# Three-term products over all 640 tokens in the dense projections of a two-layer trunk on one core

## The reference

```python
h = modulate(rms_norm(x, W['norm1_w'][l]), sh1, sc1)
# layer 0
qa, ka, va, qb, fa, fb, vb, gb = jnp.split(h @ w_in, offs, axis=-1)
...
y = jnp.concatenate([oa, ob], axis=-1) @ w_out
# layer 1
r = heads(xr @ wr)
k = heads(xk @ wk)
v = heads(xv @ wv)
...
return out.astype(h.dtype) @ wo, (s_f, s_b)
# both
x = x + gt1 * y
```

## Time and profile before

| | us |
|---|---|
| median of three runs | 2348.9 (2348.5 to 2353.81) |
| profiled execution | 2353.1 |
| its span, first to last instruction | 2351.1 |
| mean granted clock of TensorE | 0.964 |

### The profile page before, as it was taken

The page is one execution under the profiler, slowest core; times in us unless marked ns, Lnnn a source line. Parts: engine busy times, 40 slices in busy tenths (PEclk is TensorE's granted clock), DMA queues, the critical chain, the costliest instruction groups (busy, mean ns, idle before and its releaser), DMA issues. The chain is left out here.

```text
span 2351.1 us, 59242 instructions
## 1 busy us (share of the span) xinstructions
PE 2112.4 (90%) x25699; PEld 1801.1 (77%) x25699; DVE 1388.3 (59%) x2656; ACT 1033.1 (44%) x1865; POOL 310.0 (13%) x542
## 2 busy tenths in 40 slices
PE   6999878888999999989995888888887989999998
PEld 3678654578999999944874777777775889999998
DVE  3142466535757484782416787777774358475746
ACT  4242454325444444381224555565553254434353
POOL 1000230010000000100002443443342100000000
PEclk8999999989999999999996999999998999999999
DMA  7211209911122212131200000000001221222212
GB/s 273 72 68 43 75 1 326 376 59 54 54 91 72 90 57 88 36 99 60 73 17 6 7 9 6 7 9 10 9 7 41 72 72 54 90 72 72 89 56 81
DMA packets 127982, 167.78 MB, mean 71 GB/s; under 512 B 13788, under 2 KB 85228, under 8 KB 127596
## 3 DMA queue, kind: packets, MB, share of 16 engines
q1 hardware_dynamic: 127724, 164.00, 20.8%
HBM read 160.44 MB, written 3.54 MB: 70 GB/s over the span
## 5 line engine op out<-in xcount | busy, mean ns | idle before, releaser
L171 PE MATMUL psum<-arena 64*64 64x64 f32 (+6 forms) x17072 | 829.1, 248 | 131.1 <-DVE arena L2192 15.9
L171 PEld LDWEIGHTS psum<-arena 64*64 64x64 f32 (+3 forms) x17072 | 664.1, 146 | 338.6 <-issue 152.9
L171 PE MATMUL psum<-hidden_high,weights_high 128*128 128x320 f32 x896 | 281.8, 315 | 30.6 <-DVE weights_low L769 19.2
L171 PE MATMUL psum<-hidden_high,weights_low 128*128 128x320 f32 x896 | 279.0, 311 | 0.0
L171 PE MATMUL psum<-hidden_low,weights_high 128*128 128x320 f32 x896 | 278.8, 311 | 0.0
L171 PE MATMUL psum<-norm_high,weights_low 128*128 128x320 f32 x992 | 226.6, 310 | 0.0
L171 PE MATMUL psum<-norm_high,weights_high 128*128 128x320 f32 x992 | 226.6, 310 | 0.0
L171 PE MATMUL psum<-norm_low,weights_high 128*128 128x320 f32 x992 | 226.6, 310 | 0.0
L171 PEld LDWEIGHTS psum<-hidden_high,weights_high 128*128 128x128 f32 x896 | 170.0, 190 | 37.1 <-DVE weights_low L769 25.6
L171 PEld LDWEIGHTS psum<-hidden_low,weights_high 128*128 128x128 f32 x896 | 170.2, 190 | 0.0
L171 PEld LDWEIGHTS psum<-hidden_high,weights_low 128*128 128x128 f32 x896 | 169.9, 190 | 0.0
(11 more groups left out here) (229 smaller groups left out, 3381.7 us busy)
## 6 DMA issues: line engine op xcount, KB each, us to landing
weights<-in_mlp_w SPq DMA_DIRECT2D x64, 1024.0 KB, 5.3
arena<-in_ada_w SPq DMA_DIRECT2D x24, 2048.0 KB, 9.2
arena<-in_ab_w_in SPq DMA_DIRECT2D x6, 2048.0 KB, 7.8
arena<-in_ab_w_out SPq DMA_DIRECT2D x2, 2048.0 KB, 9.2
arena<-in_rwkv_wv SPq DMA_DIRECT2D x2, 2048.0 KB, 7.7
arena<-in_rwkv_wr SPq DMA_DIRECT2D x2, 2048.0 KB, 7.9
arena<-in_rwkv_wk SPq DMA_DIRECT2D x2, 2048.0 KB, 7.9
arena<-in_rwkv_wo SPq DMA_DIRECT2D x2, 2048.0 KB, 8.8
```

The source lines that it names most:

```text
L171: return nc.tensor.matmul(out, lhsT, rhs, start=start, stop=stop, skip_group_check=shared)
```

## The change

In the fast tiles, the prompt's tokens are treated as the sample's. A step over k is now six fp32r products of 320 columns, three terms for each half of the 640 tokens, in the order of the MLP's. The split activations are 640 columns wide. The high weights keep two buffers. The low weights have none of their own: DVE writes them over the raw weights, in the ring's slot (for the first block of out1, in the place where that block is loaded ahead). The finished tile lies in two halves of 320 columns in the two banks instead of 512 and 128, so the evacuations read it so, and the residual add takes three instructions (0 to 319, 320 to 511, 512 to 639) in place of two. Buffers of the splits move within the arena. The diff:

```diff
@@ -151,6 +151,12 @@
 
             return PS[:, b:b + 2, :].rearrange("p b n -> p (b n)")[:, 0:n]
 
+        def halves(b):
+            return PS[:, b:b + 2, 0:HN]
+
+        def in_halves(x):
+            return x.rearrange("p (g n) -> p g n", g=2)
+
         def con(c, n=P):
             return CON[:, c:c + n]
 
@@ -309,10 +315,10 @@
                                 pe.wait_ge(S("fast_low"), fast_of[n] + 1)
                             if x0 is not None:
                                 pe.wait_ge(S("fast_x"), x0 + k + 1)
-                            mm(PS[:, pb, 0:NS], wh[:, k, :], xh(k), start=k == 0, stop=False)
-                            mm(PS[:, pb, 0:NS], wh[:, k, :], xl(k), start=False, stop=False)
-                            mm(PS[:, pb, 0:NS], wl[:, k, :], xh(k), start=False, stop=k == kt - 1)
-                            last = mm(PS[:, pb + 1, 0:NP_], w[:, k, 128 * j:128 * j + 128], act(i, k)[:, NS:T], **se)
+                            for term, (wx, xx) in enumerate(((wh, xh), (wh, xl), (wl, xh))):
+                                for g in range(2):
+                                    last = mm(PS[:, pb + g, 0:HN], wx[:, k, :], xx(k)[:, HN * g:HN * g + HN],
+                                              start=k == 0 and term == 0, stop=k == kt - 1 and term == 2)
                         elif kind == "cm":
                             lw = w[:, k, 128 * j:128 * j + 128]
                             mm(PS[:, pb, 0:NS], lw, act(i, k)[:, 0:NS], **se)
@@ -350,17 +356,22 @@
         def pieces(name, offsets):
             return [rounded(f"{name}_w{q}", off, KT, P) for q, off in enumerate(offsets)]
 
-        IN_W = pieces("in", (42 * T + 4096, 60 * T, 60 * T + 1024, 60 * T + 2048))
-        IN_T = rounded("in_t", U_S * T, 2, NS)
-        IN_H, IN_L = rounded("in_h", U_H * T, KT, T), rounded("in_l", 42 * T, KT, NS)
-        OUT_W = [pieces("mixed0", [16 * T + 1024 * q for q in range(4)]), pieces("mixed1", [8 * T + 1024 * q for q in range(4)])]
-        OUT_H, OUT_L = ([[rounded(f"mixed{l}_{x}{k}", at + NS * k, 1, NS)[:, 0, :] for k in range(KT)] for l, at in enumerate(ats)]
-                        for x, ats in (("high", (24 * T, 24 * T + 4096)), ("low", (24 * T + 4096, 40 * T))))
-        PROJ_W = pieces("proj", (59 * T, 59 * T + 1024, 59 * T + 2048, U_RK * T + 4096, U_XI * T))
-        OMM = flat(59 * T + 3072, 48)
-        PROJ_T = rounded("proj_t", 59 * T + 3120, 1, NS)
+        IN_W = pieces("in", (60 * T, 60 * T + 1024))
+        IN_T = rounded("in_t", U_S * T, 2, T)
+        IN_H, IN_L = rounded("in_h", U_H * T, KT, T), rounded("in_l", 42 * T, KT, T)
+        OUT_W = [pieces("mixed0", [16 * T + 1024 * q for q in range(2)]), pieces("mixed1", [8 * T + 1024 * q for q in range(2)])]
+
+
+        def rows(name, *ats):
+            return [rounded(f"{name}{q}{k}", at + T * k, 1, T)[:, 0, :] for q, (at, n) in enumerate(ats) for k in range(n)]
+
+        OUT_H = [rows("mixed0_high", (16 * T + 2048, KT)), rows("mixed1_high", (42 * T, KT))]
+        OUT_L = [rows("mixed0_low", (24 * T + 2048, KT)), rows("mixed1_low", (8 * T + 2048, 4), (24 * T + 4096, 4))]
+        PROJ_W = pieces("proj", (59 * T, 59 * T + 1024))
+        OMM = flat(59 * T + 2048, 48)
+        PROJ_T = rounded("proj_t", 59 * T + 2096, 1, T)
         PROJ_H = [rounded(f"proj_h{q}", (U_XI + 8 * q) * T, KT, T) for q in range(2)]
-        PROJ_L = [rounded("proj_l0", U_RK * T, KT, NS), rounded("proj_l1", U_H * T, KT, T)]
+        PROJ_L = [rounded("proj_l0", U_RK * T, KT, T), rounded("proj_l1", U_H * T, KT, T)]
         fast_x0, x0 = {}, 0
         for name in FAST:
             fast_x0[name] = x0
@@ -370,15 +381,27 @@
 
             q = fast_of[n] - fast_first[name]
             x0 = fast_x0[name] if q == 0 else None
+            wl = fast_low_in_place(n)
             if name == "in":
-                return IN_W[q % 2], IN_W[2 + q % 2], lambda k: IN_H[:, k, 0:NS], lambda k: IN_L[:, k, :], x0
+                return IN_W[q % 2], wl, lambda k: IN_H[:, k, :], lambda k: IN_L[:, k, :], x0
             if name == "proj":
                 half = q // 8
                 x0 = fast_x0[name] + KT * half if q % 8 == 0 else None
-                return PROJ_W[q % 2], PROJ_W[2 if q % 2 == 0 else 3 + half],                     lambda k: PROJ_H[half][:, k, 0:NS], lambda k: PROJ_L[half][:, k, 0:NS], x0
-            w = OUT_W[int(name[-1])]
+                return PROJ_W[q % 2], wl, lambda k: PROJ_H[half][:, k, :], lambda k: PROJ_L[half][:, k, :], x0
             l = int(name[-1])
-            return w[q % 2], w[2 + q % 2], lambda k: OUT_H[l][k], lambda k: OUT_L[l][k], x0
+            return OUT_W[l][q % 2], wl, lambda k: OUT_H[l][k], lambda k: OUT_L[l][k], x0
+
+        LOW_RING = [rounded(f"ring_low{q}", RING + SLOT * q, KT, 512) for q in range(2)]
+        LOW_RING2 = [rounded(f"ring_low_short{q}", RING + SLOT * q, KT, 256) for q in range(2)]
+        LOW_OUT1 = rounded("out1_low", U_RK * T, KT, 512)
+
+        def fast_low_in_place(n):
+
+            _n, i, j = fast_n[fast_of[n]]
+            name = next(x for x in FAST if first_tile[x] <= n < first_tile[x] + sum(len(b[3]) for b in stages[x]))
+            b = first_block[name] + i
+            x = LOW_OUT1 if b == first_block["out1"] else (LOW_RING if stages[name][i][2] == 512 else LOW_RING2)[b % 2]
+            return x[:, :, 128 * j:128 * j + 128]
 
         def fast_raw(f):
             n, i, j = fast_n[f]
@@ -927,14 +950,14 @@
             H = unit(U_H, 8)
             for k in range(KT):
                 dve.wait_ge(S("norm_out"), k + 1)
-                step(V.tensor_copy(IN_T[:, k % 2, :], H[:, k, 0:NS]))
-                V.tensor_tensor(IN_L[:, k, :], H[:, k, 0:NS], IN_T[:, k % 2, :], ALU.subtract).then_inc(S("in_split"), 1)
+                step(V.tensor_copy(IN_T[:, k % 2, :], H[:, k, :]))
+                V.tensor_tensor(IN_L[:, k, :], H[:, k, :], IN_T[:, k % 2, :], ALU.subtract).then_inc(S("in_split"), 1)
             f0 = fast_first["in"]
             fast_low(dve, f0)
             dve.wait_ge(S("in_split"), KT)
             dve.wait_ge(S("tile_product"), fast_n[f0][0])
             for k in range(KT):
-                V.tensor_copy(IN_H[:, k, 0:NS], H[:, k, 0:NS]).then_inc(S("fast_x"), 1)
+                V.tensor_copy(IN_H[:, k, :], H[:, k, :]).then_inc(S("fast_x"), 1)
             n0 = first_tile["in"]
             fast_low(dve, f0 + 1)
             for n in range(n0 + 11, n0 + 31):
@@ -951,10 +974,10 @@
                     V.tensor_scalar(unit(x), unit(x), LB[:, 5, p:p + 1], LB[:, 4, p:p + 1], ALU.mult, ALU.add)
                 elif i >= 23:
                     dve.wait_ge(S("gate_sigmoid"), i - 22)
-                    V.tensor_tensor(unit(x), pair(2 * (n % 2)), unit(U_S + n % 2), ALU.mult).then_inc(S("tile_evacuated"), 1)
+                    V.tensor_tensor(in_halves(unit(x)), halves(2 * (n % 2)), in_halves(unit(U_S + n % 2)), ALU.mult).then_inc(S("tile_evacuated"), 1)
 
         def out_x(name, k):
-            return unit((U_MIX if name == "out0" else U_R) + k)[:, 0:NS]
+            return unit((U_MIX if name == "out0" else U_R) + k)
 
         def residual_dve(dve, name, gate):
             ADA = ADAS[:, int(name[-1]), :, :]
@@ -968,9 +991,9 @@
             for n, _, (_, j, m) in tile_list(name):
                 dve.wait_ge(S("tile_product"), n + 1)
                 pb = 2 * (n % 2)
-                for g, (t0, c) in enumerate(GROUPS):
-                    x = X[:, m, t0:t0 + c]
-                    ins = V.scalar_tensor_tensor(x, PS[:, pb + g, 0:c], ADA[:, gate + m, g:g + 1], x, ALU.mult, ALU.add)
+                for half, g, t0, t1 in ((0, 0, 0, HN), (1, 0, HN, NS), (1, 1, NS, T)):
+                    x, c0 = X[:, m, t0:t1], t0 - HN * half
+                    ins = V.scalar_tensor_tensor(x, PS[:, pb + half, c0:c0 + t1 - t0], ADA[:, gate + m, g:g + 1], x, ALU.mult, ALU.add)
                 ins.then_inc(S("tile_evacuated"), 1)
                 if fast_of[n] + 2 < f0 + 8:
                     fast_low(dve, fast_of[n] + 2)
@@ -999,11 +1022,13 @@
                 if gated(x) and kind == "cm":
                     if n - first_gated >= 2:
                         act.wait_ge(S("tile_evacuated"), n - 1)
-                    A.activation(unit(U_S + n % 2), pair(pb), ACT.Sigmoid).then_inc(S("gate_sigmoid"), 1)
+                    A.activation(in_halves(unit(U_S + n % 2)), halves(pb), ACT.Sigmoid).then_inc(S("gate_sigmoid"), 1)
                     if n + 2 in fast_of and fast_raw(fast_of[n + 2])[0] == name:
                         fast_high(act, fast_of[n + 2])
                     continue
-                if kind == "cm":
+                if n in fast_of:
+                    ins = A.activation(in_halves(unit(x)), halves(pb), func(x))
+                elif kind == "cm":
                     ins = A.activation(unit(x), pair(pb), func(x))
                 else:
                     dst, c = tm_dst(kind, j, x)
@@ -1643,11 +1668,11 @@
 
         def mix_split(dve, step, s, k):
 
```

(6 more changed lines are left out.)

## The result

The changed kernel takes 2335.45 us (median of four runs, 2334.78 to 2338.42) against 2348.7 of the kernel before, measured beside it: ratio 0.9941, 95% interval 0.9924 to 0.9958. That is 13.3 us less. The forecast was 2334, within 2327 to 2342. The profiled execution took 2338.42 us, which beside the 2353.1 of before is 14.7 us less, and the prediction's sum for it was 2338.5.

The account below looks back on a forecast made before the run. PE, busy 90% of the span, was taken as the bound. -15.5 + 0.07 + 0.3 + 2 x (0.13 + 0.13) = -14.6 us took the profiled 2353.1 to 2338.5 and the median 2348.9 to 2334.3, range 2327 to 2342.

Parts of the forecast that it names:

- The step: Dense tiles of in, out0, out1, proj: a step over k falls from 0.917 to 0.880 us, 15.5 us in 424 steps.
- The first subtraction of the output stages: Out0 and out1: PE's first product waits for DVE's split of 640 columns, 0.819 us against 0.684, costing 0.13 us a stage.
- The last evacuation: End of out0 and out1: the residual add in three instructions costs +0.13 us a stage, upper end +0.30.
- chain of keys and queries: Stage in: norm and rotary work delays low weights, costing 0.3 us; rival with eight tiles held loses 2.3, within 0.88 chance.
- a wait of 0.9 us: Stage in near 153 us: PE's wait for a low weight tile, 0.61 us before, was to grow by 0.29 us.
- The first rounding copy: Stage in: the copy PE waits for grows with 640 columns in place of 512, costing 0.07 us.
- The slack of the sixth mix: Proj: DVE's sixth mix ends before tile 8 needs its data; the room shrinks from 6.0 to 4.9 us, cost 0.
- Low weights over the raw ones: Fast tiles: DVE's subtraction, writing over raw weights in the ring, keeps its 1.22 us; cost 0.
- Weight loads set the pace: Fast tiles: six loads of 0.19 us make a step 1.14 us, 94 us longer in all, 2443; chance 0.04.
- threshold of 152.8 ns: Fast tiles: the product interval, 0.917/6, from which the rival of weight loads setting the pace decides.
- The estimate of 20.5 us: Fast tiles: gain if the skill page's intervals held, steps 0.815 and 0.863 us, in place of 15.5; not in the sum.
- Clock falls at other places: MLP gaps and scan: falls of 0.8 us each dealt anew, forecast 2332 to 2338, with scan 2328 to 2342; within 0.88 chance.

## Why the prediction was right

**The step.** 424 x (0.917 - 0.880) = 15.5 us was the one large term. The step measured 0.880 us, the interval of the products was that of the MLP to the last digit. By stage: in lost 5.9 us (forecast 168 x 0.0367 - 0.07 - 0.3 = 5.8), proj's tiles 4.5 to 4.7 (4.7), out0 2.4 and 1.5 in two profiles, out1 2.1 and 3.1 (2.1 each). The run with the old form in both output stages bears out their part by its stage lengths: 4.6 us, for a forecast of 4.2. That the profiled execution took 2338.42 us for a forecast of 2338.5 is luck: unchanged stretches of two profiles of one kernel differ by up to 2.5 us. The fair comparison is 13.3 us by the medians, with an interval of about 10 to 18, for 14.6.

**The small costs.** The first subtraction of the output stages, 821 ns for 684, is 0.14 us (0.13 said). The last evacuation grew by 0.13 us, the value taken between 0 and 0.30. PE's first product of out0 comes 0.14 us later after the stage's start. The tile over which the chain of keys and queries lies gave none of its 0.29 us, as the sum had it; the sign that I named for it, a wait of 0.9 us, did not come: 0.69 us are recorded. The first rounding copy, 487 ns against 419 or so, is 0.07 us. The slack of the sixth mix is 4.9 us, as worked out.

**Low weights over the raw ones.** Cost 0, shown for the output stages by the run with buffers of their own: the same load, the same subtraction, the same step.

**Weight loads set the pace (the slower rival).** They don't at 320 columns: at 256 the products are still closer. But the rival was not empty, only its price was wrong: it took a load for 0.19 us, its recorded length, where loads follow each other 0.108 to 0.112 us apart. The kernel with 512 and 128 columns shows what that costs where the product over a load is shorter: 0.14 us a step, 59 us in 424 steps, and its time is 61 us above the changed kernel's. It was right to reject the rival from the MLP's rows, whose products have the same width. Its threshold of 152.8 ns was not reached, but the 6 ns between it and 146.7 are the whole gain. The Trainium skill, TensorE: Matmul & The Clock Gate, section LDWEIGHTS (loading the stationary operand), gives a load P/1.2 ns, 107 for 128 columns. The traces agree: loads start 108 ns apart at the least with 512 and 128 columns, and products 111.5 ns apart with 192; the 188 to 192 ns of the load's records don't agree with it. The records overlap like the products' do. The formula N/2.4 + 2.5 ns that the prediction quotes from the Trainium skill (same page, section Back-to-back issue gap) is given in that section for isolated products, not for a stream with a load each. The estimate of 20.5 us applies it to such a stream, and the trace doesn't agree: at 320 columns 146.7 ns were measured and not 135.8.

**Clock falls at other places.** They do move, at seven of eight places between two profiles of the same kernel. The prediction had the size of one fall wrong: 0.8 us, from a stretch that ended in the middle of the fall. Of the trace of before, the next stretch, and PE's products where the fall begins and ends:

```profile
2080.00:2090.00 10.00, 10.00 (x64) 0.91 0.29 95
...
2078.38 0.44 PE L171 MATMUL psum<-hidden_high,weights_low 128*128 128x320 f32 x1
...
2081.82 0.31 PE L171 MATMUL psum<-hidden_high,weights_high 128*128 128x320 f32 x1
```

Between these two starts are 13 products in 3.44 us, 1.91 at 0.1467 each: the fall costs 1.5 us. At that price the prediction's own reckoning gives 2330 to 2342 us from the gaps of the MLPs, and 2325 to 2349 with the same again from the scan, which is wider than the range of 2327 to 2342 that it named. The sum leaves the falls as they were, so the forecast of 2334 doesn't hang on their price; that the measured time lies so close to it is in part luck. Four of the eight gaps fell in either profile of the changed kernel for three before. What the falls did to the difference of 13.3 against 14.6 us isn't known; both lie within the scatter of the runs.

**The chain of keys and queries** held the gain of one tile, 0.29 us, at 7.04 us a tile, as the sum had it. At 4.7 us a tile it and the low weights behind it held 4.7 us of 49, part of it through a fall of the clock.

## What to carry to other kernels

When a new stream of products replaces an old one on a full TensorE, the best price is the distance between starts of the same shapes elsewhere in the same profile; durations of single records are about twice too long (309 ns for a product every 147), since products and loads overlap. Splitting columns evenly matters: 320 and 320 gained 0.6%, 512 and 128 lost 1.9% with the same columns and loads, because a weight load is hidden only under a product that is long enough, here 0.11 us. A fall of the granted clock is priced over a stretch that holds the whole fall. Buffers can be saved by writing a derived operand over its source once nothing reads the source; in the two output stages this cost nothing.

## What the runs showed of the hardware

- The interval of fp32r products with a load each, at full clock: 0.229 us at 512 columns, 0.1467 at 320, 0.120 at 256, 0.1115 at 192 and 0.112 at 128. A straight line in the columns holds down to 256, and a floor below it; at half clock the floor is 0.213 us.
- The floor is that of the weight loads. With 512 and 128 columns in turn, loads start 0.108 and 0.232 us apart in proj, while a long product is recorded 0.060 us behind a short one. Every product here has a load of its own, also where the weight stays the same, so no run shows what a product without one would take.
- One fall of the granted clock at a gap of the MLP cost 1.5 us: 13 products of 320 columns in 3.44 us in place of 1.91.
- With nearly all fast products at 128 columns the granted clock stayed at 0.50 through the products of out0 and out1 (one run), although PE was recorded as busy 10.00 of 10 us. With less arithmetic it took 2352 us, 89 more than the kernel with 192 columns.
